# Dealing the projection blocks beside the stick-breaking units in proportion to key blocks instead of evenly

## What is computed

```
u = rmsnorm(x) @ w_in                     # 1024 columns each for qb, kb, vb, zb
for each head, for each block of 128 queries (block number b = 0..3):
    z       = q_blk @ k[: (b+1)*128].T * scale          # 128 x (b+1)*128
    log_1mb = where(key < query, log_sigmoid(-z), 0)
    after   = reverse cumulative sum of log_1mb, less itself
    A       = where(key < query, exp(log_sigmoid(z) + after), 0)
    out     = A @ v[: (b+1)*128]
yb = out * silu(zb)
y  = concat(ya, yb) @ w_out
```

## Time and profile before

| | us |
|---|---|
| median of three runs | 2022.13 |
| the profiled execution | 2020.71 |
| its span, first to last instruction | 2019.0 |
| the stick-breaking steps, first scores to last block | 1433.6 to 1639.7 |

### The profile page before, as it was taken

How to read it: one execution, slowest core, us unless ns; L and a number is a source line. 1 busy time by engine, 2 the same in 40 slices (tenths; PEclk the granted TensorE clock), 3 DMA queues, 4 the chain that set the end, 5 groups by cost and what they waited for, 6 DMA issues and landing times.

```text
span 2019.0 us, 25217 instructions
## 1 busy us (share of the span) xinstructions
PE 1956.5 (97%) x9056; PEld 1617.4 (80%) x9056; DVE 758.5 (38%) x1184; ACT 785.1 (39%) x1537; POOL 844.0 (42%) x654
## 2 busy tenths in 40 slices
PE   7999999999999999999998999999999999999898
PEld 5777888988887888888886887888787778888787
DVE  4211322440222322222347764312376646015743
ACT  5322443413424433333364443143446535333332
POOL 3523444415354355444342643344333343445452
PEclk9999999999999999999998999999999999999999
DMA  4522333313133223222231422233222231322231
GB/s 140 151 63 71 96 84 84 87 39 110 62 114 111 73 99 110 96 96 94 78 94 42 114 84 63 57 96 91 64 68 74 68 130 62 106 94 89 89 105 52
DMA packets 98583, 176.90 MB, mean 88 GB/s; under 512 B 10747, under 2 KB 16519, under 8 KB 98492
## 3 DMA queue, kind: packets, MB, share of 16 engines
q1 hardware_dynamic: 94212, 170.17, 27.2%
q10 hardware_dynamic: 4280, 5.51, 0.9%
HBM read 171.70 MB, written 3.93 MB: 87 GB/s over the span
## 4 chain that ended last, share of the span: by engine, by line
issue 46%; PE 31%; POOL 20%; DVE 2%; ACT 1%; POOLq 1%; ACTq 0%; DVEq 0%
POOL w_lo L567 20%; PE proj L1735 10%; PE proj L1737 10%; PE proj L1736 10%; DVE arena L1717 1%; ACT arena L814 1%; POOLq L571 0%; DVE act_lo L1148 0%; PE work L1869 0%; DVE arena L1721 0%; POOLq L569 0%; ACT arena L647 0%; DVE arena L1720 0%; PE work L1870 0%; ACT w_hi L843 0%
## 5 line engine op out<-in xcount | busy, mean ns | idle before, releaser
L567 POOL TENSOR_TENSOR w_lo<-w_raw,w_hi 128x512 fp32r<-128x512 f32 x632 | 838.6, 1345 | 1147.0 <-ACT w_hi L592 1007.5
L1735 PE MATMUL proj<-act_hi,w_hi 128*128 128x512 f32 (+1 forms) x1264 | 494.9, 392 | 10.3 <-DVE arena L1450 2.3
L592 ACT CAST w_hi<-w_raw 128x512 fp32r<-128x512 f32 x536 | 313.3, 618 | 479.8 <-PE proj L1737 465.8
L1736 PE MATMUL proj<-act_lo,w_hi 128*128 128x512 f32 (+1 forms) x1264 | 487.3, 385 | 0.0
L1737 PE MATMUL proj<-act_hi,w_lo 128*128 128x512 f32 (+1 forms) x1264 | 486.9, 385 | 0.0
L1735 PE MATMUL proj<-w_hi,act_hi 128*128 128x512 f32 x800 | 321.2, 402 | 9.4 <-DVE arena L1702 4.9
L1737 PE MATMUL proj<-w_hi,act_lo 128*128 128x512 f32 x800 | 312.9, 391 | 0.0
L1736 PE MATMUL proj<-w_lo,act_hi 128*128 128x512 f32 x800 | 312.8, 391 | 0.0
L1735 PEld LDWEIGHTS proj<-act_hi,w_hi 128*128 128x128 f32 x1264 | 238.9, 189 | 62.5 <-POOL w_lo L567 7.3
L1737 PEld LDWEIGHTS proj<-act_hi,w_lo 128*128 128x128 f32 x1264 | 238.8, 189 | 48.1
L1736 PEld LDWEIGHTS proj<-act_lo,w_hi 128*128 128x128 f32 x1264 | 239.0, 189 | 46.1 <-issue 0.5
(11 more groups left out here) (303 smaller groups left out, 1803.5 us busy)
## 6 DMA issues: line engine op xcount, KB each, us to landing
w_raw<-in_w_in SPq DMA_DIRECT2D x154, 256.0 KB, 2.8
w_raw<-in_w_in_ab SPq DMA_DIRECT2D x146, 256.0 KB, 2.6
w_raw<-in_w_mlp SPq DMA_DIRECT2D x128, 256.0 KB, 2.7
w_raw<-in_w_in_c SPq DMA_DIRECT2D x64, 256.0 KB, 2.7
w_raw<-in_w_out_ab SPq DMA_DIRECT2D x32, 256.0 KB, 2.6
w_raw<-in_w_out_c SPq DMA_DIRECT2D x32, 256.0 KB, 2.9
w_raw<-in_w_o_gla SPq DMA_DIRECT2D x16, 256.0 KB, 2.8
w_raw<-in_w_out SPq DMA_DIRECT2D x16, 256.0 KB, 2.6
```

Of the source, the lines that this page charges most:

```text
L567: return pool.tensor_tensor(w_lo[:, slot, :], w_raw[:, slot, :], w_hi[:, slot, :].bitcast(F32), ALU.subtract)
L592: act.copy(w_hi[:, b % RING, :], w_raw[:, b % RING, :]).then_inc(hi_ready, 1)
L1735: pe.matmul(out_, a_hi, b_hi, start=first, stop=False)
L1736: pe.matmul(out_, a_hi, b_lo, start=False, stop=False)
```

## The change

`beside` is dealt by another function. Step i gets a share in proportion to 2 + (i - 1) % 4: 5 where i % 4 is 0, 2 where it is 1, 3 where it is 2, 4 where it is 3. That is 2 plus the place, 0 to 3, of unit i-1 (the unit whose weights are turned in step i) among its head's query blocks. The order of the blocks stays.

```
-        beside = spread(slabs[by_name["sb_q"][1].at:by_name["even_out0"][1].at + 1], SB_STEPS + 1)
+        def spread_by_keys(group, n):
+
+            todo = [(s, j) for s in group for j in range(s.n)]
+            keys = [2 + (i - 1) % MT for i in range(n)]
+            upto = [len(todo) * sum(keys[:i]) // sum(keys) for i in range(n + 1)]
+            return [todo[upto[i]:upto[i + 1]] for i in range(n)]
+
+        beside = spread_by_keys(slabs[by_name["sb_q"][1].at:by_name["even_out0"][1].at + 1], SB_STEPS + 1)
```

## The result

The changed kernel takes 2031.9 us in the median of seven runs (2028.69 to 2034.08). The kernel before, run again beside it, takes 2023.01 (2020.83 to 2024.91, seven runs). The ratio is 1.0042, with a 95% interval of 1.003 to 1.0054: about 8.5 us slower by the ratio, 8.9 by the medians. The profiled execution of after is 2030.37 us, 9.7 above that of before. The forecast was 2028.5, with a range up to 2031.5.

The account below looks back on a forecast made before the run. TensorE was taken as the bound, with the ScalarE-VectorE chain a nearly equal runner in this stage. V(31) 5.3 us late plus 1.1 for `gated` made 6.4: 2027.1 profiled, 2028.5 against the median, range 2024.1 to 2031.5.

Parts of the forecast that it names:

- Step 16's three blocks: Three blocks ahead of T(15); copy(15) holds Exp(16) in ScalarE's queue, so the chain is 6.4 us late.
- V(31) got 2.7 back: Stage end: one block instead of two ahead of V(31) gives back 2.77 us, so V(31) comes 5.3 late.
- units 17 to 31: The chain paces; shifted roundings and a covered S(22) wait give back 0.9, step 28 adds 2.5; T(31) 8.0 us late.
- Step 28: Repeats step 8: third block, copy(27) behind T(27), Exp(28) behind copy(27); plus 2.5 us.
- the price of the boundary: Step 15: first sb_z block waits 4.4 us for ScalarE's copies behind log_terms(15); TensorE 5.6 late, 5.3 at T(14).
- Behind the stage: After the turning of sb_o nothing is moved and TensorE paces again, so the lateness stays: nothing added.
- The covered stalls win: Rival: the chain keeps its old times and all 5.1 us of covered TensorE stalls are gained; 2017.5 us, chance 0.04.
- Boundary only: Rival: step 15's wait comes, but third blocks in steps 8 and 28 cost nothing; about 2024.2 us, chance 0.20.
- The dealing changes nothing that matters: Rival: the stage is elastic enough for blocks differing by one in 16 of 35 steps; 2022.1 us, chance 0.03.
- The third rounding: Rival: third subtractions cost units 6, 14 and 26 up to 1.3 us each, all `gated` slow; 2032.4 us, chance 0.12.
- The slow `gated`: Stage end: `gated` products beside GpSimd's subtractions cost 1.1 to 2.3 us more; forecast took 1.1, the 0.12 rival the upper end.

Follow-up runs that it names:

- the third blocks alone: Kernel before with a third block in steps 8 and 28, taken from 9 and 29, all else as before: 2025.16 us (1.0011).
- both waits filled: Changed kernel with idle matmuls ahead of the first block of each sb_z, 17 in step 15 and 9 in step 25: 2028.91 us (1.0036).
- the covers alone: Kernel before with a second block only in steps 12, 20 and 32, taken from 13, 21 and 33: 2020.49 us (0.9992).
- the boundary alone: Kernel before with the last block of sb_v moved from step 14 to step 15, all else as before: 2026.78 us (1.0019).
- the third block of step 16 alone: Kernel before with one block moved from step 17 into step 16, steps 14 and 15 as before: 2024.26 us (1.0011).
- the boundary taken out: Changed kernel with the last block of sb_v put back into step 14, all else as changed: 2025.93 us (1.0022).
- one wait filled: Changed kernel with 17 idle matmuls between the last block of sb_v and the first of sb_z: 2028.39 us (1.0035).

## Why the prediction was wrong by size

**Direction and mechanism.** Slower was right, and so was the place of every term, up to the first block of sb_z. Exp(8) was 1.5 late (forecast 1.7), Exp(9) 1.9 (2.1), Exp(14) 1.9 (1.8). TensorE waited 4.04 us at the boundary (4.27 from start to start, less the usual 0.23; forecast 4.4). Step 16's three blocks and copy(15) ahead of Exp(16) acted as said. V(31) got 2.7 back (2.77), and `gated` took 1.2 more (1.1).

**Luck** is in the part between, units 17 to 31. The sum is near, the lateness grew by 1.8 from Exp(16) to T(31) (forecast 0.9 back and 2.5 more, together 1.6), but its parts are not. The lateness first rose from 8.0 to 9.4 at Exp(18), which the forecast does not have, and was back at 8.3 at Exp(25): 0.3 more in place of 0.9 less. Step 28 then added 1.5 and not 2.5, in after as in the kernel with the third blocks alone (1.0 late at Exp(25), 2.5 at T(31)). Two errors of 1.2 and 1.0 cancel, and the 8.15 against 8.0 of the kernel with both waits filled owes something to that.

**The step that failed** is the price of the boundary. I booked 4.4 us of waiting and went on to "5.3 at T(14)", with the block behind the wait at its usual 2.77 us. The block took 4.4 us, 1526.38 to 1530.79, since the clock had fallen to half behind the wait. T(14) was 6.8 late. This is the 1.6 that the two filled waits took away again. The forecast counts waits by their length alone; none of its terms or rivals has a clock in it, though the rows of before could show that it matters, since outside the stage before has stretches at 0.50 as well (3.41 us at 1912.5, for one). The Trainium skill (TensorE: Matmul & The Clock Gate, section HAM oscillation — how this bites in real kernels) tells of a kernel in which a wait between bursts of matmuls takes the clock down again each time, and its cost comes on top of the wait; by that rule, the trace agrees at this wait, and the forecast would have been about 1.6 higher. It does not agree at every wait of the stage: behind 2.40 us before T(31) in before and 2.40 us in step 25 of after the clock stayed at 1.00.

**Behind the stage** I booked zero and the profile has 1.5. This is the clock again, at two waits of TensorE for VectorE that stand at the same places in every kernel here. The first is 1.86 us long, 55 us behind the turning of sb_o. TensorE's timeline and the table by stretch, first of before, then of after:

```profile
1694.88 0.39 PE L1735 MATMUL proj<-act_hi,w_hi 128*128 128x256 f32 x1 [1.86 <-DVE arena L1665]
1694.90:1708.00 13.10, 11.37 (x92) 10.97 (x93) 9.51 (x13) 8.51 (x18) 8.37 (x6) 1.00 0.36 119
```

```profile
1703.18 0.39 PE L1742 MATMUL proj<-act_hi,w_hi 128*128 128x256 f32 x1 [1.86 <-DVE arena L1672]
1704.70:1707.90 3.20, 3.20 (x17) 3.20 (x17) 3.20 (x3) 2.38 (x7) 2.34 (x2) 0.50 0.54 166
```

Counted from the turning of sb_o, after is 0.1 late at this wait and 0.9 at the next one, 13 us on. The second place is a wait of 4.85 us (at 1912.62 in before, at 1921.63 in after). The granted clock is 0.50 for 3.41 us there in before and for 6.83 us in after, which makes 0.9 into 1.5. The other profiles bear this out: a half clock at the first place (in seven of the 13 kernels) costs 0.7 to 0.85, 6.83 us instead of 3.41 at the second costs 0.7 to 1.2, and where the turning doesn't wait for `gated` the next slab starts 0.8 earlier. Nothing is moved at these places. That the shift of the stage decides which of them loses the clock is argued, not shown: no run moved the start alone.

**The whole.** For the profiled execution the forecast was 2027.1 and the profile has 2030.37. Of these 3.3 us the stage has 1.7 (the clock) and the rest of the program 1.5. From the profiled execution to the median I added 1.4, and it was 1.5. The measured time is 0.4 above the range; either of the two terms would account for that. The median of before, 2022.13 when the forecast was made, is 2023.01 over the seven runs beside after; against those the change is 8.5 to 8.9 us, where the forecast said 6.4.

**The rivals.** *The covered stalls win*: no; the covers alone pay 1.9 us at the turning of sb_o, all of it from step 32, and nothing from T(11), T(19) and V(18). *Boundary only*: no; the third blocks of steps 8 and 28 cost 2.5 at T(31) and that of step 16 1.55, each alone. *The dealing changes nothing that matters*: no; the interval is clear of 1. *The third rounding*: no. VectorE's timelines of unit 6, the last of its five operations, show what the third subtraction costs, first in after, then in before:

```profile
1473.64 0.59 DVE L1605 TENSOR_TENSOR arena<-arena,before_neg 128x128 f32<-128x128 f32 x1
```

```profile
1473.23 0.29 DVE L1598 TENSOR_TENSOR arena<-arena,before_neg 128x128 f32<-128x128 f32 x1
```

That is 0.3 us for unit 6, and the same for units 14 and 26, near the zero that I took and far below 1.3. What I said against that rival holds: only the short last operation meets it. The rule of the Trainium skill on the port (SBUF — State Buffer, section Who interferes with whom) is not hurt by this, since it tells that two operations exclude each other, not that the second has much left when the third subtraction comes. *The slow `gated`*: 1.2 and not 2.3 more. Three of the four products took 1.77 us and the first 0.85, against 1.85, 1.77, 0.68 and 0.68 in before, so the low end of three slow products was right.

**What stays open** is when a wait lowers the clock. The lengths here are those in the brackets of the rows. Before T(31) the wait is 2.40 us in before, in the boundary alone and in the third block of step 16 alone; the first keeps the clock and the other two lose it. The wait of step 25 is 2.4 us in after, in the covers alone, in the kernel with the boundary taken out and in that with one wait filled; the first two keep it, the others lose it. The wait of 1.86 us behind the stage lost it in seven of 13 kernels. So between 1.86 and 2.41 us length alone does not decide. Every longer wait that these profiles show from S(0) on was followed by a half clock or ended in one: 3.23 us in the third blocks, 3.45 in the boundary alone, 3.88 in after, and the 4.85 us behind the stage in all 13.

All of this is read from one profiled execution per kernel. Other executions can have their half clocks elsewhere: those of one kernel lie up to 8 us apart, and the time goes with the clock. Of the 82 executions of before that stand beside the experiments, the 7 with a mean granted clock of 0.990 took 2025.0 us in the mean, the 8 with 0.995 took 2019.3.

## What to carry to other kernels

Where two runners of about equal length share a stage, a covered stall pays only on the one that sets the end there: of three covers one paid. Before blocks are dealt in another way, look at which steps get the border between two slabs: the emptying of the banks stands at a fixed place in another engine's program, and a block that crosses a step's border can end up waiting for all of it. And a wait of TensorE of about two us or more in an otherwise full stage should be priced twice, once as it is and once with 1.6 us on top, with both ends in the range.

## What the runs showed of the hardware

The granted clock went to 0.50 behind single waits of 1.9 to 3.9 us, in a stage where TensorE is otherwise at work almost all the time, and each such stretch of 3.41 us cost about 1.6 us there. Not each such wait did it: of equal waits of 2.40 us some were followed by it and some were not. With seventeen matmuls without a use in the place of the wait the clock stayed at 1.00, and the half clock was then found behind a later wait; with both filled the stage had none.

Four products of VectorE took 5.98 us beside GpSimd's subtractions and 2.50 us without them, a factor of 2.4, and where GpSimd's run could be put behind them it cost nothing that the rows show.
